# Function tables of ScalarE loaded by hand in a two-block transformer kernel

## The reference

```python
def mixer_block(u, ...):                      # block 1
    z = u @ w_in                              # 2048 -> 11264 columns, split into hq hf hi hg aq ak av gates
    f = sigmoid(hf)
    g = lb + (1.0 - lb) * f
    log_g = log(g)                            # decays of the gated scan, 8 heads
    q = silu(hq) * HG_DK ** -0.5
    o = hgrn2_scan(q, 1.0 - g, hi, log_g)     # uses exp of sums of log_g
    y_a = rms_norm(o, hg_norm_w) * silu(hg)
    y_b = chunk_band_attention(aq, ak, av, rel_bias)      # softmax, 16 heads
    gate_a, gate_b = split(sigmoid(gates), 2)
    return (gate_a * (y_a @ w_branch_a) + gate_b * (y_b @ w_branch_b)) @ w_out

h = x + mixer_block(rms_norm(x, norm_mix_w), ...)
h = h + square(relu(rms_norm(h, norm_mlp_w) @ w_up)) @ w_down
# block 2
proj = rms_norm(h, norm_mix) @ w_in_2         # uv, qkv, gates
v = layer_norm(gelu(v));  y_a = gelu(u) * (w_s @ v + b_s)
y_b = neighbourhood_attn(q, k, v, rpb)        # softmax
h = h + (gate_a * (y_a @ wb[:1024]) + gate_b * (y_b @ wb[1024:])) @ w_out_2
gate, val = split(conv3(rms_norm(h) @ w_up_2), 2)
h = h + (silu(gate) * val) @ w_down_2
return rms_norm(h, norm_final)
```

## Time and profile before

| | |
|---|---|
| median of three runs | 3032.91 us |
| the profiled execution, its own time | 3035.66 us |
| its span, first to last instruction | 3033.9 us |
| TensorE busy | 2901.6 us, 96% |
| VectorE busy | 2170.2 us, 72% |
| ScalarE busy | 1524.8 us, 50% |
| TensorE's granted clock, mean over the span | 0.992 |
| one table load on ScalarE | 1283 ns |

### The profile page before, as it was taken

How to read it: one execution, slowest core, us unless ns; L and a number is a source line. 1 busy time by engine, 2 the same in 40 slices (tenths; PEclk the granted TensorE clock), 3 DMA queues, 4 the chain that set the end, 5 groups by cost and what they waited for, 6 DMA issues and landing times.

```text
span 3033.9 us, 50114 instructions
## 1 busy us (share of the span) xinstructions
PE 2901.6 (96%) x16379; PEld 2480.3 (82%) x16379; DVE 2170.2 (72%) x3324; ACT 1524.8 (50%) x2293; POOL 133.9 (4%) x138
## 2 busy tenths in 40 slices
PE   5999999989999999999998999999999999999997
PEld 4787877778788888888887878788788888888886
DVE  5777777777667776766786666667767887778775
ACT  5555555556454444444454544445555455545554
POOL 1000000000000000000040000000010000000001
PEclk9999999999999999999998999999999999999999
DMA  5555555545666666666664556565565666666663
GB/s 166 150 150 156 150 151 149 151 140 173 175 186 188 185 189 180 186 189 184 186 198 136 165 154 176 155 176 165 168 188 168 182 192 188 185 184 193 193 189 114
DMA packets 1016023, 519.68 MB, mean 171 GB/s; under 512 B 28980, under 2 KB 1014700, under 8 KB 1015596
## 3 DMA queue, kind: packets, MB, share of 16 engines
q1 hardware_dynamic: 1014032, 513.90, 59.1%
q10 hardware_dynamic: 1820, 3.65, 0.3%
HBM read 515.35 MB, written 2.13 MB: 171 GB/s over the span
## 4 chain that ended last, share of the span: by engine, by line
PE 65%; DVE 17%; issue 9%; ACT 7%; DVEq 1%; DMA 0%; ACTq 0%; SPq 0%; POOL 0%; POOLq 0%
PE acc L399 29%; PE acc L401 14%; PE psT L399 6%; PE psX L399 6%; DVE w_lo L1120 5%; ACT w_hi L736 4%; PE psX L401 3%; PE psT L401 3%; DVE work L1126 1%; DVE probs L1184 1%; DVE HS L1243 1%; ACT probs L782 1%; DVE soft L1185 1%; DVE work L1132 1%; DVE HS L1252 1%
## 5 line engine op out<-in xcount | busy, mean ns | idle before, releaser
L1120 DVE TENSOR_TENSOR w_lo<-w_raw,w_hi 128x1024 fp32r<-128x1024 f32 (+1 forms) x960 | 1171.9, 1226 | 592.1 <-ACT w_hi L736 531.0
L736 ACT ACTIVATE w_hi<-w_raw 128x1024 fp32r<-128x1024 f32 (+1 forms) x960 | 1003.2, 1052 | 666.8 <-PE acc L401 513.0
L399 PE MATMUL acc<-XU,w_hi 128*128 128x512 f32 x3488 | 1243.7, 399 | 6.7 <-DVE work L1126 6.0
L401 PE MATMUL acc<-XU,w_lo 128*128 128x256 f32 x3488 | 977.1, 280 | 0.0
L399 PEld LDWEIGHTS acc<-XU,w_hi 128*128 128x128 f32 x3488 | 656.0, 188 | 169.6 <-DVE w_lo L1120 6.7
L399 PE MATMUL acc<-XY,w_hi 128*128 128x512 f32 x2112 | 762.3, 403 | 26.2 <-DVE work L1126 10.3
L401 PEld LDWEIGHTS acc<-XU,w_lo 128*128 128x128 f32 x3488 | 659.0, 189 | 1.1
L401 PE MATMUL acc<-XY,w_lo 128*128 128x256 f32 x2112 | 595.9, 282 | 0.0
L399 PEld LDWEIGHTS acc<-XY,w_hi 128*128 128x128 f32 x2112 | 400.6, 190 | 131.3 <-DVE w_lo L1120 14.0
L401 PEld LDWEIGHTS acc<-XY,w_lo 128*128 128x128 f32 x2112 | 403.3, 191 | 0.1
L399 PE MATMUL psT<-XY,w_hi 128*128 128x512 f32 x632 | 225.9, 398 | 4.7 <-DVE w_lo L1120 4.2
(11 more groups left out here) (248 smaller groups left out, 2624.2 us busy)
## 6 DMA issues: line engine op xcount, KB each, us to landing
w_raw<-in_w_in SPq DMA_DIRECT2D x320, 512.0 KB, 4.0
w_raw<-in_w_up SPq DMA_DIRECT2D x300, 512.0 KB, 4.2
w_raw<-in_w_down SPq DMA_DIRECT2D x208, 512.0 KB, 4.0
w_raw<-in_w_out SPq DMA_DIRECT2D x64, 512.0 KB, 3.9
w_raw<-in_w_branch SPq DMA_DIRECT2D x32, 512.0 KB, 3.7
w_raw<-in_w_branch_a SPq DMA_DIRECT2D x16, 512.0 KB, 3.8
w_raw<-in_w_branch_b SPq DMA_DIRECT2D x16, 512.0 KB, 3.8
bias<-in_rel_bias SPq DMA_DIRECT2D x8, 384.0 KB, 6.3
```

Of the source, the lines that this page charges most:

```text
L399: nc.tensor.matmul(bank[:, :], hi[:, k, col:col + P], X[:, k0 + k, :], start=first and k == 0, stop=False, skip_group_check=True)
L401: done = nc.tensor.matmul(bank[:, 0:T], lo[:, k, col:col + P], X[:, k0 + k, 0:T], start=False, stop=last and k == nk - 1, skip_group_check ...
L736: act.activation(w_hi[s][:, 0:n], w_raw[s][:, 0:n], ACT.Copy).then_inc(hi_done, 1)
L1120: V.tensor_tensor(w_lo[s][:, 0:n], w_raw[s][:, 0:n], w_hi[s][:, 0:n].bitcast(F32), ALU.subtract).then_inc(lo_dve, 1)
```

## The change

The change touches ScalarE's stream alone. `act.preload_act_table(F)` writes an `ACT_TABLE_LOAD` of a table that has function `F`, at this place in the stream; `act.preload_act_table_set(LOG_EXP)` loads the table `natural_log_exp_and_others`, which has logarithm and exponential. The functions that follow then find their table loaded, and the build adds no load. No other engine's instructions change, and no semaphore does.

```diff
+        LOG_EXP = "natural_log_exp_and_others"
...
+            act.preload_act_table_set(LOG_EXP)
             act.wait_ge(stat_done, 1)
             rstd(rs[:, :], psS[:, 0:T], D, eps_rms, rs1[:, :], rs_ready)
...
                         copy_cross(p, i, t, b, acc_first if t == 0 else acc[(t - 1) % 2])
+                    if b == 0:
+                        act.preload_act_table(ACT.Sigmoid)
                     if b == 1:
                         sigmoid_of(2, "hq_z", "hq_sig", i)
...
                     if b == 5:
                         act.wait_ge(S("g_ready"), i + 1)
                         sigmoid_of(3, "hg_z", "hg_sig", i)
+                        act.preload_act_table(ACT.Ln)
                         act.activation(wk(0), wk(0), ACT.Ln).then_inc(S("lg_ready"), 1)
+                        act.preload_act_table_set(LOG_EXP)
...
             def branches(name, X):
                 p, x = ph[name], name[-1]
+                act.preload_act_table(ACT.Sigmoid)
                 act.wait_ge(S(f"gates_z{x}"), HEADS)
...
             out_projection("out1", XY, 1, C_MLP1)
+            act.preload_act_table_set(LOG_EXP)
             act.wait_ge(stat_done, 2)
...
             ffn1("ffn1last", 0)
+            act.preload_act_table_set(LOG_EXP)
             next_operand(ph["ffn1last"], KD - 1)
...
+            act.preload_act_table(ACT.Gelu_apprx_tanh)
             p = ph["gmv"]
...
+            act.preload_act_table_set(LOG_EXP)
             act.wait_ge(S("gv_sq_used"), HEADS)
...
+                    if b == 0:
+                        act.preload_act_table(ACT.Gelu_apprx_tanh)
                     if b == 1:
                         act.wait_ge(S("u_z"), i + 1)
                         act.activation(wk(0), wk(0), ACT.Gelu_apprx_tanh).then_inc(S("u_ready"), 1)
+                        act.preload_act_table_set(LOG_EXP)
...
             out_projection("out2", XU, 3, C_FFN2)
+            act.preload_act_table_set(LOG_EXP)
             act.wait_ge(stat_done, 5)
...
+            act.preload_act_table(ACT.Silu)
             ffn2("ffn2first", 0)
             with act.Fori(0, ph["ffn2"].iters) as i:
                 ffn2("ffn2", i)
+            act.preload_act_table_set(LOG_EXP)
             ffn2("ffn2last", 0)
```

## The result

The changed kernel takes 3045.90 us (median of 13 executions, 3032.64 to 3051.78), the kernel before 3034.57 us (13, 3029.07 to 3043.67). The ratio is 1.0032, with a 95% interval of 1.0019 to 1.0045: slower by 0.32%, some 10 us. The forecast was 3034 us, no change, with a range up to 3044. It was wrong by 12 us, and the measured time lies just outside the range.

A forecast was written before the change was run, and what follows sets the result against it. The prediction took TensorE, busy for 96% of the span, and its waits on ScalarE as the bound. From 3035.66 us, -1.4 without the clock, -4.5 and +6.8 for the clock gave 3036.6, or 3034 against the median; range 3023 to 3044.

The forecast's parts named there:

- What bounds the kernel: Whole kernel: TensorE is busy 96% of the span; a load counts only where a TensorE wait hangs on ScalarE.
- the load on the chain: Head loop: exponentials' load between logarithm and first rounding lengthens the L472 wait by 1.40 us an iteration, 11.2 in eight.
- The L460 wait: Head loop: TensorE's 3.0 us of waiting for the logarithms goes, as two loads leave block 21.
- +8.2: Head loop without the clock: 11.2 us for added loads less 3.0 for the L460 wait, within -3.0 and +11.2.
- The gains outside: Outside the head loop: branch1 -1.7, branches -4.6, psT -0.5, gmv -1.5, the end -1.3 us, plus -4.5 of clock.
- -4.5 of clock: Shorter long waits at 678, 772, 1615 and in branch2 give back 1.7, 1.0, 0.5 and 1.3 us, within 0 and -9.
- 1.7 us at `branch1`: Entry of branch1: VectorE starts L1290 1.7 us earlier, so TensorE's 3.30 us wait shrinks to 1.6, with no clock fall expected.
- At `branch1`, `gmv` and `psT`: TensorE's waits: 3.30 us at branch1 shrinks to 1.6, 5.53 before gmv by 1.5, 0.5 at psT goes.
- three waits of TensorE in a head iteration: Head loop: TensorE waits at L460 (3.0 us in 7 of 8), L472 (1.05 each) and L495 (2.9 each).
- the two branches: Second iteration of each branches loop: removed loads shorten the final wait by 2.3 us, -4.6 in all, bounds 0 and -5.2.
- The clock in the head loop: 16 waits of 2.4 to 3 us may each bring a 1.7 us fall, 0 to +27; four taken, +6.8 us.
- The slower rival: Head loop: clock falls in most iterations after L472 and L495 waits; twelve falls give +14.5, 3047 us; chance 0.20.

The follow-up runs named there:

- the filled kernels: Kernel before with idle matmuls in TensorE's two head-loop waits, 3031.69 us; the same with the exponentials' load moved behind the logarithm, 3042.80 us.
- The kernel with the edits outside alone: Changed kernel's hand-placed loads outside the head loop only, head loop as in the kernel before: 3020.43 us, ratio 0.9960 to the kernel before.
- the load at block 8: Changed kernel with the exponentials' load moved to block 8, right ahead of the first exponential: 3030.74 us, ratio 0.9980 to the kernel before.
- the load alone: Kernel before with one edit, the exponentials' load placed by hand between logarithm and roundings: 3056.67 us, ratio 1.0073.
- one table: Changed kernel with LOG_EXP loaded ahead of the decays' logarithm and no load behind it: 3025.88 us, ratio 0.9969 to the kernel before.
- only L472 filled: Changed kernel with 8 idle matmuls ahead of the lg_lo wait, the tile_pairs wait left idle: 3041.42 us, ratio 1.0028 to the kernel before.
- three loads: Changed kernel with two further table loads behind the decays' logarithm: 3071.70 us, ratio 1.0127 to the kernel before.
- the one with the load and both waits filled: Kernel before with the exponentials' load moved behind the logarithm, plus 8 and 10 idle matmuls in TensorE's two head-loop waits: 3042.80 us, ratio 1.0042.

## Why the prediction was wrong

**What bounds the kernel, and the load on the chain: right.** The forecast price was 1.40; the L472 wait shows 1.43, the filled kernels 1.44. The L460 wait went as forecast. Net, the head loop with the clock held takes (555.74 - 549.16) / 7 = 0.94 us more an iteration, 7.5 us in all, where +8.2 stood in the sum.

**The gains outside: right in sum, in part by luck.** The forecast was -9.6 us of waits and loads and -4.5 of clock, -14.1. The kernel with the edits outside alone, which lacks the 1.7 us at `branch1`, measured -12 (-17 to -7), where -10.5 was expected. The clock part of it is 0.9931 against 0.9911, -6, but it did not come where it was forecast. In the changed kernel's profile the fall at `branch1` is still there (row 697 to 703), behind the wait at `gmv` the clock is as before (0.61 over 1617 to 1625 us, 0.59 over 1614 to 1622 before), and at `out1` it gives back 0.6 us (0.79 over 789 to 797, 0.72 over 773 to 781). Two falls of 1.7 us are gone for which the prediction had no gain: at 1595 us (0.79 in the earlier trace rows, 1.00 over 1598 to 1606 now) and near 2965 (0.83 over 2960 to 2970, 1.00 over 2958 to 2968 now). At `branch1`, `gmv` and `psT` the waits came out as forecast. In two readings it slipped without harm to the sum. It counts three waits of TensorE in a head iteration; the list has a fourth of that size, L460 for VectorE's L1132, 8.9 us in 8, which is 9.0 in the changed kernel. And the two branches were read as alike, -2.3 each, and were -3.1 and -1.1; why the second gained less I have not followed.

**The clock in the head loop: this step failed.** The prediction put it: "The eight L495 waits brought none, the 2.92 did; nearest to the new waits are the eight. I take four falls, +6.8 us." It took the behaviour of eight waits for evidence on how a wait of this length behaves. But they were eight copies of one case: the same wait, in a loop whose every turn took 78.4 to 78.7 us. Their number said nothing on what they would do once the turn had another length. In every kernel in which the turn changed and a wait of 2.9 us stayed (the load at block 8, the load alone, one table, only L472 filled, three loads), falls appear in the head loop, six to fifteen in the profiled execution; in the profiles of before and of the one with before's head loop none. Nine showed in the changed kernel's. Over all executions the changed kernel stands 0.0056 of clock below the one with before's head loop and the same edits outside, which is 17 us or ten falls of 1.7.

With that size the terms close: +7.5 for the load, -12 for the edits outside, -1.7 at `branch1`, and +11 to +17 for the falls (by 1.4 us of length for each of eight, or by the clock) is +5 to +11, against the measured +9.7 (5.8 to 13.7). The slower rival, twelve falls and 3047 us, was the right mechanism at nearly the right size; it was given 0.20 where the range of 0 to 16 falls, with nothing to choose by, should have given it and the forecast about the same.

**Still open.** What makes one wait of 2.9 us bring a fall and another not. The pattern over the kernels goes with the length of the turn, but none of them varied this length alone with everything else kept, so this is an inference, not shown. That the idle time in the waits is the cause of the falls is shown, since filling it removes them (two pairs by the ratios: changed kernel 18.5 us, one table 9 us), and that the loads as such are not is shown by the one-table kernel, which has fewer of them than before and eight falls.

## What to carry to other kernels

Where a load by hand stands decides what it costs: off the chain no cost could be told here (the load at block 8 against one table, 0.9980 against 0.9969 with overlapping intervals), and on the chain that releases TensorE it costs its 1.3 to 1.4 us each time, so look for the one table that serves all functions in between before placing two. When an edit changes the length of a loop's turn, do not take a clock that stood at 1.00 behind a wait of 2 to 3 us for a property of the wait, and price a fall for each such wait. Filling such waits with idle matmuls took the falls away here and cost nothing measurable where there were none.

## What the runs showed of the hardware

TensorE has two paces at the full clock, and it was not expected. The rows are the matmuls of 1200 to 1600 us, in the middle of the feed-forward part with the granted clock at 1.00 in both kernels; columns are count, busy us, mean ns of one, idle us before them. Before, then changed:

```profile
L399 PE MATMUL acc<-XU,w_hi 128*128 128x512 f32 x312 | 111.5, 399 | 0.0
...
L401 PE MATMUL acc<-XU,w_lo 128*128 128x256 f32 x312 | 87.6, 281 | 0.0
```

```profile
L399 PE MATMUL acc<-XU,w_hi 128*128 128x512 f32 x320 | 112.2, 392 | 0.0
L401 PE MATMUL acc<-XU,w_lo 128*128 128x256 f32 x320 | 89.0, 278 | 0.0
```

From the starts of the L399 in these stretches, less the few gaps over 0.4 us, a pair of matmuls (L399 and L401) takes 0.3533 us in the one and 0.3467 in the other. The stretch holds 2236 matmul records in the kernel before and 2290 in the changed one, both at a clock of 1.00 (windows, columns as in the earlier trace rows, before and then changed):

```profile
1200.00:1600.00 400.00, 396.66 (x2236) 343.50 (x2235) 296.89 (x440) 184.24 (x251) 37.74 (x32) 1.00 0.66 190
```

```profile
1200.00:1600.00 400.00, 397.18 (x2290) 348.09 (x2289) 297.19 (x441) 186.10 (x250) 32.60 (x27) 1.00 0.66 191
```

The change touches nothing there, and other kernels have the two paces in other stretches (between 1500 and 1600 us the one with only L472 filled and the one with the load and both waits filled have 0.3467, the one with three loads 0.3533), each held for a hundred microseconds and more. Over 400 us that is 7.5 us. It shows in the positions: from the start of `out1` to the end of the first feed-forward part the kernel before took 1595.46 - 772.75 = 822.7 us, the changed one 1601.06 - 789.04 = 812.0:

```profile
1601.06 0.50 PE L399 MATMUL acc<-XY,w_hi 128*128 128x512 f32 x1 [3.36 <-DVE hT L1343]
```

Together with the gains outside, this is why the changed kernel's profiled execution is as short as that of before in spite of entering `branch1` 18 us later (696.31 against 678.13). Something other than the mean clock makes executions of one kernel differ: two of the changed kernel, at 3032.64 and 3051.78 us, both have 0.989. The two paces may be it, but only one execution of each kernel has a trace, so this is not shown. What sets the pace was not tried. For reading a pair of profiles it means: compare stretch by stretch with their waits, and take totals from many executions.
